# Part of a depthwise convolution moved between engines, with its diagonal weights loaded instead of built

## The reference

```python
z = h @ w_in
cv_v, cv_g, lr_x, lr_y, q, k, v, g_lr, og = split(z)
u = cv_v * sigmoid(cv_g)
u = causal_dw_conv(u, conv_dw_w, conv_dw_b)        # 256 channels, 31 taps
u = silu(layer_norm(u, conv_ln_g, conv_ln_b))
r = rg_lru(...) * gelu(lr_y)                       # a scan over time
o = gla_chunked(q, k, v, lg)                       # 4 heads, chunks of 64
o = rms_norm(o, gla_norm_g) * silu(og)
return concatenate([u, r, o]) @ w_out
```

## Time and profile before

| | us |
|---|---|
| median of three runs | 2743.56 |
| lowest and highest | 2742.04, 2745.74 |
| the profiled execution | 2746.38 |
| its span, from first to last instruction | 2744.6 |
| TensorE busy | 2668.8 (97%) |
| VectorE busy | 2007.4 (73%) |
| ScalarE busy | 1472.0 (54%) |
| GpSimd busy | 192.6 (7%) |

### The profile page before, as it was taken

One profiled execution on the slowest core, in us unless ns is written; L12 is line 12 of the kernel. 1 busy time (PEld: TensorE's weight loads), 2 busy tenths in 40 slices (PEclk: granted clock), 3 DMA queues, 4 the chain that ended last, 5 costly groups with the idle time before them and its releaser, 6 DMA issues.

```text
span 2744.6 us, 46143 instructions
## 1 busy us (share of the span) xinstructions
PE 2668.8 (97%) x15974; PEld 2316.1 (84%) x15974; DVE 2007.4 (73%) x2985; ACT 1472.0 (54%) x2290; POOL 192.6 (7%) x70
## 2 busy tenths in 40 slices
PE   5999899998999999999999999999999999999999
PEld 3766778887999877788899987999887888899987
DVE  7755699998998576743799847899466653699954
ACT  3253489986554356743555525555346753555532
POOL 1441124430000000000000000000000000000000
PEclk9999899999999999999999999999999999999999
DMA  7740599993332241123233232332232123323232
GB/s 287 277 144 31 190 336 412 412 393 115 107 98 89 99 161 57 51 78 114 93 108 104 86 115 79 109 105 90 96 117 106 53 76 109 100 93 107 92 100 100
DMA packets 95470, 376.63 MB, mean 137 GB/s; under 512 B 10800, under 2 KB 11072, under 8 KB 93120
## 3 DMA queue, kind: packets, MB, share of 16 engines
q1 hardware_dynamic: 89584, 348.69, 35.7%
q0 software_dynamic: 4320, 15.73, 1.4%
q10 hardware_dynamic: 1456, 10.74, 1.0%
HBM read 363.59 MB, written 15.73 MB: 138 GB/s over the span
## 4 chain that ended last, share of the span: by engine, by line
PE 84%; DVE 7%; issue 4%; ACT 3%; DMA 0%; POOL 0%; ACTq 0%; DVEq 0%; POOLq 0%
PE pb L1456 15%; PE pb L1458 15%; PE pb L1457 15%; PE pb L1901 10%; PE pb L1903 10%; PE pb L1902 10%; PE pb L2092 1%; PE pb L2124 1%; PE pb L2048 1%; PE pb L1535 1%; ACT SP L1338 1%; DVE hid L2846 1%; PE pb L2101 1%; DVE SP L3023 0%; PE pb L1740 0%
## 5 line engine op out<-in xcount | busy, mean ns | idle before, releaser
L1901 PE MATMUL pb<-bl,g_wh 128*128 128x256 f32 x2464 | 701.9, 285 | 11.0 <-DVE bl L2757 6.9
L1902 PE MATMUL pb<-bh,g_wl 128*128 128x256 f32 x2464 | 697.8, 283 | 0.0
L1903 PE MATMUL pb<-bh,g_wh 128*128 128x256 f32 x2464 | 697.8, 283 | 0.0
L1901 PEld LDWEIGHTS pb<-bl,g_wh 128*128 128x128 f32 x2464 | 473.3, 192 | 15.9 <-issue 9.7
L1902 PEld LDWEIGHTS pb<-bh,g_wl 128*128 128x128 f32 x2464 | 473.6, 192 | 1.6 <-issue 1.4
L1903 PEld LDWEIGHTS pb<-bh,g_wh 128*128 128x128 f32 x2464 | 473.5, 192 | 0.0
L2796 DVE TENSOR_TENSOR w_lo<-raw,w_hi 128x1024 fp32r<-128x1024 f32 x160 | 195.5, 1223 | 186.3 <-ACT w_hi L699 185.2
L1456 PE MATMUL pb<-hl,w_hi 128*128 128x512 f32 x688 | 285.6, 415 | 13.4 <-DVE hl L2255 9.8
L699 ACT ACTIVATE w_hi<-raw 128x1024 fp32r<-128x1024 f32 x186 | 195.9, 1057 | 189.3 <-PE pb L1458 175.4
L1458 PE MATMUL pb<-hh,w_hi 128*128 128x512 f32 x688 | 269.9, 392 | 0.0
L1457 PE MATMUL pb<-hh,w_lo 128*128 128x512 f32 x688 | 269.9, 392 | 0.0
(11 more groups left out here) (488 smaller groups left out, 5551.6 us busy)
## 6 DMA issues: line engine op xcount, KB each, us to landing
raw<-in_wstream SPq DMA_DIRECT2D x220, 512.0 KB, 3.3
m_raw<-in_moe_stream SPq DMA_DIRECT2D x96, 512.0 KB, 8.7
g_own<-in_gu_stream SPq DMA_DIRECT2D x44, 768.0 KB, 4.2
raw<-in_gu_stream SPq DMA_DIRECT2D x44, 768.0 KB, 4.2
m_first<-in_moe_stream SPq DMA_DIRECT2D x48, 512.0 KB, 7.1
hf<-in_moe_stream SPq DMA_DIRECT2D x48, 512.0 KB, 6.6
ada_ring<-in_ada SPq DMA_DIRECT2D x8, 2048.0 KB
g_own<-in_gu_stream SPq DMA_DIRECT2D x44, 256.0 KB, 3.1
```

What stands on the lines that cost most here:

```text
L1901: pe.matmul(o, lh, rl, start=first and k == 0, stop=False, skip_group_check=True)
L1902: pe.matmul(o, ll, rh, start=False, stop=False, skip_group_check=True)
L1903: m = pe.matmul(o, lh, rh, start=False, stop=k == 3, skip_group_check=True)
```

## The change

- VectorE now does 21 taps of the second tile instead of 18. They stand in five groups (3, 5, 5, 4, 4, `EARLY`) right behind the modulation's last step, while the input projection is still running, and no longer behind the states. `PE_TAPS` gives TensorE ten.
- Between the groups VectorE makes the four low halves of pairs 9 and 10, which GpSimd made.
- The 41 diagonals come ready from DRAM, `conv_diag`, made on the host as a layout of the weights. The sync queue loads them to `diag` between the chunks of pairs 9 and 10. GpSimd builds none.
- TensorE does one tap of the second tile between the two key-value groups, six (up to `FILL`) behind the second, none between the heads, one between the last two head statistics and two behind the last.
- The first sum over the channels with ones moves from in front of the output projection into its first tile, behind three of that tile's seven columns.

```diff
-PE_TAPS = (CONV_K, 13)
-DIAG = tuple((t, k) for t in range(NU) for k in range(0, PE_TAPS[t], TAPS))
+PE_TAPS = (CONV_K, 10)
+FILL = 7
+N_DIAG = sum(PE_TAPS)
+EARLY = (3, 5, 5, 4, 4)
...
-            stream((ADA - ADA1) // ADA_EACH, C_WOUT // 2 + 1)
+            n_ada = (ADA - ADA1) // ADA_EACH
+            stream(n_ada, n_ada + 2)
+            sp.wait_ge(ada_used, n_ada)
+            sp.dma_start(diag[:, 0:N_DIAG, :], conv_diag).then_inc(diag_ready, 16)
+            stream(n_ada + 2, C_WOUT // 2 + 1)
...
             low(j0, 1)
-            for i, (j, s) in enumerate(((j0 + 1, 0), (j0 + 1, 1), (j0 + 2, 0))):
-                diagonals(i, i + 1)
-                low(j, s)
-            diagonals(3, len(DIAG))
-            low(j0 + 2, 1)
             pool.wait_ge(xh_ready, 1)
...
                 if p == 1:
+                    pe.wait_ge(conv_out, 1)
+                    conv(1, 0, 1)
                     pe.wait_ge(sc_ready, 2)
...
-            pe.wait_ge(conv_out, 1)
-            conv(1, 0, TAPS)
+            conv(1, 1, FILL)
...
                 m.then_inc(gla_mm, 1)
-                conv(1, TAPS + h, TAPS + h + 1)
                 if h >= 1:
                     head_rms(h - 1)
-            conv(1, TAPS + GH, PE_TAPS[1])
+            conv(1, FILL, FILL + 1)
             head_rms(GH - 1)
+            conv(1, FILL + 1, PE_TAPS[1])
...
-            for t in range(NU):
-                pe.wait_ge(conv_out, t + 1)
-                m = pe.matmul(pb[0][:], ones, z[:, Z_CG + t, :], start=t == 0, stop=t == NU - 1)
-            m.then_inc(ln_mm, 1)
             pe.wait_ge(o_ready, GH)
...
-                out_tile(i, range(1, KD))
+                if i == 0:
+                    out_tile(0, (1, 2, 3))
+                    pe.wait_ge(o_root, 1)
+                    for t in range(NU):
+                        pe.wait_ge(conv_out, t + 1)
+                        m = pe.matmul(pb[0][:], ones, z[:, Z_CG + t, :], start=t == 0, stop=t == NU - 1)
+                    m.then_inc(ln_mm, 1)
+                    out_tile(0, range(4, KD))
+                else:
+                    out_tile(i, range(1, KD))
...
+            dve.wait_ge(u_ready, 2)
+            k = PE_TAPS[1]
+            for i, n in enumerate(EARLY):
+                taps(k, n)
+                k += n
+                if i < 4:
+                    j, half = C_WOUT // 2 - 2 + i // 2, i % 2
+                    dve.wait_ge(w_lod, 2 * j + half)
+                    dve.wait_ge(w_hid, 2 * j + half + 1)
+                    dve.tensor_tensor(w_lo[half][:], raw[half][:], w_hi[half][:].bitcast(F32), ALU.subtract).then_inc(w_lod, 1)
```

More of the change, by code:

```diff
@@ L189, with build @@
     ("ident", P), ("ones", P), ("pairs", P), ("upto", P), ("iota", P), ("chunk_mask", T)])
-def build(nc, xT, cond, ada, wstream, gu_stream, vecs, lvecs, const, masks, lru_gates, gla_gate, moe_stream, na_bias, sw_bias, h_rows, y_rows, out):
+def build(nc, xT, cond, conv_diag, ada, wstream, gu_stream, vecs, lvecs, const, masks, lru_gates, gla_gate, moe_stream, na_bias, sw_bias, h_rows, y_rows, out):
     ctx = ExitStack()
@@ L648, in put @@
                                         ).then_inc(y_out, 16)
-            def diagonals(first, end):
-                for t, k in DIAG[first:end]:
-                    n, w = CONV_K * t + k, min(TAPS, PE_TAPS[t] - k)
-                    pool.tensor_tensor(diag[:, n:n + w, :], ident.unsqueeze(1).broadcast_to([P, w, P]),
-                                       V("conv_w", n, w).unsqueeze(2).broadcast_to([P, w, P]), ALU.mult).then_inc(diag_ready, 1)
             j0 = C_WOUT // 2 - 3
@@ L659, in _ @@
             low(j0, 0)
-            pool.wait_ge(con_in, 16)
-            pool.wait_ge(vec_in, 48)
-            pool.wait_ge(ada_used, (ADA - ADA1) // ADA_EACH)
             low(j0, 1)
-            for i, (j, s) in enumerate(((j0 + 1, 0), (j0 + 1, 1), (j0 + 2, 0))):
-                diagonals(i, i + 1)
-                low(j, s)
-            diagonals(3, len(DIAG))
-            low(j0 + 2, 1)
             pool.wait_ge(xh_ready, 1)
@@ L1532, in conv @@
                 for k in range(first, end):
-                    if k % TAPS == 0 or k == first:
-                        pe.wait_ge(diag_ready, -(-CONV_K // TAPS) * t + k // TAPS + 1)
                     m = pe.matmul(pb[7][:], diag[:, CONV_K * t + k, :], u_pad[:, t, k:k + T], start=k == 0, stop=k == CONV_K - 1,
@@ L1540, in _ @@
             pe.wait_ge(u_ready, 2)
+            pe.wait_ge(diag_ready, 16)
             conv(0, 0, TAPS_1)
@@ L2331, in _, with taps @@
             dve.tensor_tensor(shifted_w, router_w, modv[:, 32:32 + KD].unsqueeze(2).broadcast_to([P, KD, 20]), ALU.mult).then_inc(mod_ready, 1)
+            def taps(first, n):
+                for k in range(first, first + n):
+                    u, w = u_pad[:, 1, k:k + T], V("conv_w", CONV_K + k)
+                    if k == PE_TAPS[1]:
+                        ins = dve.tensor_scalar(hidf[:], u, w, None, ALU.mult)
+                    else:
+                        ins = dve.scalar_tensor_tensor(hidf[:], u, w, hidf[:], ALU.mult, ALU.add)
+                    if k == CONV_K - 1:
+                        ins.then_inc(u_ready, 1)
+                    else:
+                        step(ins)
+            dve.wait_ge(u_ready, 2)
[8 more added lines that the diff above has]
+                    dve.tensor_tensor(w_lo[half][:], raw[half][:], w_hi[half][:].bitcast(F32), ALU.subtract).then_inc(w_lod, 1)
             dve.wait_ge(consts_or_ov_c_mm, 1)
@@ L2403, in _ @@
             dve.tensor_tensor(mt[:, 0:NR, :], mt[:, 0:NR, :], z[:, Z_LY:Z_LY + NR, :], ALU.mult).then_inc(lru_ready, 1)
-            def tap(k):
-                return u_pad[:, 1, k:k + T], V("conv_w", CONV_K + k)
-            step(dve.tensor_scalar(hidf[:], *tap(PE_TAPS[1]), None, ALU.mult))
-            for k in range(PE_TAPS[1] + 1, CONV_K):
-                ins = dve.scalar_tensor_tensor(hidf[:], *tap(k), hidf[:], ALU.mult, ALU.add)
-                if k == CONV_K - 1:
-                    ins.then_inc(u_ready, 1)
-                else:
-                    step(ins)
             dve.wait_ge(lru_ready, 2)
@@ L3291, in lay_out @@
     gg = head_pad(a["gla_w_gate"][0], DK, GH, 64).reshape(16, 2, P)
-    return dict(cond=a["c"], ada=ada_c.transpose(3, 0, 2, 1).reshape(P, ADA, D),
+    taps = np.zeros((P, N_DIAG, P), f)
+    for t in range(NU):
+        for k in range(PE_TAPS[t]):
+            taps[np.arange(P), CONV_K * t + k, np.arange(P)] = a["conv_dw_w"][0][k, P * t:P * t + P]
+    return dict(cond=a["c"], conv_diag=taps, ada=ada_c.transpose(3, 0, 2, 1).reshape(P, ADA, D),
                 xT=a["x"][0].T.reshape(KD, P, T).transpose(1, 0, 2), wstream=ws, gu_stream=gu_stream, vecs=vecs, lvecs=lv, const=con,
```

## The result

| | before | after |
|---|---|---|
| median of 20 executions each, us | 2742.76 | 2750.06 |
| lowest and highest | 2740.13, 2746.22 | 2736.58, 2752.94 |
| ratio | | 1.002, 95% interval 1.0014 to 1.0026 |
| span of the profiled execution | 2744.6 | 2746.7 |
| its mean granted clock | 0.991 | 0.987 |

The account below looks back on a forecast made before the run. It took two chains ending within 0.05 us at the output projection, TensorE's and the last head's through ScalarE and VectorE, as the bound. Projection -4.8 and ones +1.7 gave -3.1 us: 2740.5 us from 2743.56, range 2736.8 to 2745.0.

Parts of the forecast that it names:

- item 1: VectorE's taps under the projections: 21 at 0.785 us plus four low halves end at 164.7, hidden; no gain by itself.
- (2): Four low halves moved from GpSimd to VectorE under the projections: ready before TensorE's tiles want them, cost 0.
- (3): 41 diagonals by DMA, 2.69 MB in 8.6 us: cost 0; at single-chunk pace 16.9 us and a 2.5 us stall.
- (4): One tap in the 0.52 us wait before the second key-value group: costs 0.87, so TensorE +0.39 us.
- item 5: Four taps fewer behind the second key-value group, 0.87 each: -3.49 us; the wait for the states stays closed by 0.7.
- the clock as an unknown: Granted clock 0.50 in the first expert's products: a shifted rise changes seven matmuls, plus or minus about 1 us.
- (6): Two products with ones leave the line before the output projection, 2.24 us from there: TensorE ready at 238.6.
- (7): Last head ready at 239.1: TensorE waits 0.5 us, and the output projection starts 4.8 us earlier.
- The bound with 1.9: Upper bound in us of the wait before the output projection, if the last head's square pushed ScalarE's pair once.
- (8): Products with ones inside the projection's first tile still cost 1.72 us; following VectorE and ScalarE work fits behind twelve matmuls.
- The rivals: For the whole kernel: more gain, 2737.6 us, chance 0.16; nothing arrives, 2743.6, 0.14; slower, 0.06.
- The slower one: Under the projections VectorE fails to keep the tiles' pace, TensorE waits: up to 2753.3 us; chance 0.06.

Follow-up runs that it names:

- e4: Before with only the upstream part: 18 early VectorE taps, four low halves on VectorE, 44 diagonals by DMA; TensorE's order unchanged. 2743.56 us, ratio 0.9992 to 1.0009.
- e1: After with three taps moved back behind the first three heads, two from in front, one from between the last statistics. 2742.34 us, ratio 0.9994 to 1.0017.
- e2: Before with its four taps from between the heads moved: one before the last head statistic, the others behind it. 2750.29 us, ratio 1.0008 to 1.0033.
- e7: After with two useless tap-size products added behind each of the first three heads. 2746.17 us, ratio 1.0011 to 1.0029.
- e5: After with its ten TensorE taps rearranged: four behind the second key-value group, one inside each of four heads, one behind the last statistic. 2742.19 us.
- e6: After with an eleventh TensorE tap: five behind the second key-value group, one behind each of four heads, one behind the last statistic. 2744.33 us.
- e8: After with its ten TensorE taps rearranged: five behind the second key-value group, one inside each of the first three heads, one last. 2742.54 us.
- e10: After with an eleventh TensorE tap: five behind the second key-value group, one inside each of four heads, one behind the last statistic. 2743.54 us.
- e9: Same as e8, but the first products with ones back in front of the output projection. 2738.63 us, ratio to before 0.9975 to 0.9993.
- e12: After with only the first products with ones put back in front of the output projection; heads still bare. 2749.44 us, ratio 1.0011 to 1.0031.
- e3: After with one useless tap-size product added behind each of the first three heads. 2743.44 us, ratio 0.9997 to 1.0015.

## Why the prediction was wrong

**VectorE's taps (item 1): right.** 0.78 a tap for 0.785. VectorE waits 7.14 behind them, where the end at 164.7 in front of 171.8 meant 7.1.

**Low halves (2) and diagonals (3): right at cost 0.** TensorE has no wait under the projections. The transfer took 9.8 us for the 8.6 that I had put, between the two ends, nearer to the cheap one, and neither ScalarE nor TensorE waited for what was queued behind it. e4 shows the sum of the three (with 18 taps for 21), 0 within 0.09%.

**The tap in the wait (4): right.** The wait of 0.52 is gone, and the second group starts 1.88 after the first. Before it was 0.82 and the wait, about 1.4; so +0.48 for +0.39. The states behind it were no bound in after, as item 5 said with 0.7 us to spare: in e1, with two taps less in front of the heads, TensorE waits 0.87 for them.

**Four taps fewer (5), at 0.87 each: here it failed.** The number was right for the taps and wrong for what was between them. They stood in the heads, whose own rows I left at the price of the earlier trace rows without a word on why the price should hold: the sum put the effect of the bare heads on the clock at nothing. Without the taps the granted clock fell to 0.50 in most executions (16 of 20 by the mean clock), and a block then took 1.50 for 0.87, 10.4 us over the heads and what stands behind them. Bare blocks aren't dear by themselves: after's first and all those in e2's trace, with the clock up, take 0.87. The prediction named the clock as an unknown, but looked for it only in the first expert's products, where a 0.50 stood in the trace already. The stretch at 0.50 by the router is there in every trace, and the distance from the second use of the ones to the first expert keeps its length (83.71, 83.81).

**The ones leave the line (6), and what is late next (7): right where the clock is up.** The wait in front of the projection was 0.36 in after and in e7, for the 0.5 of the sum. The bound with 1.9 is what e5, e6, e8 and e10 have, 1.74 and 1.75, since one tap instead of two is left behind the last statistic to cover the last head, and ScalarE's pair is pushed by the one before it.

**The ones inside (8): right in the arithmetic.** In e7, at full clock, the sum of all items is -2.9 for the -3.1 forecast. But the choice was the wrong one of two: with the last head late the ones in front fill its wait, 35.85 in e9 for 37.65 in e8. In after's own order the difference is small: the wait they would fill is 0.36, and e12 is 0.37 shorter than after, both with the clock down.

**The rivals.** The slower one had 0.06 and the wrong mechanism: VectorE kept the pace. None of the rivals was that the removal of a tap could slow the products around it. The four executions of after with a mean clock of 0.990 or more have a median of 2742.8, that of before; four that lie 8.6 us apart neither show nor refute the forecast's gain, which rests on e7's trace. Of the range, the upper end counted scatter of 1.4 us above no gain, from three runs of before; after's own executions lie 16 us apart.

## What to carry to other kernels

A product that is taken out from between small ones isn't worth its own duration alone: ask what the small ones cost without it, and whether the trace of before has any stretch of the same kind that stands bare. Where filler work has to be cut, cut it in front of or behind a sparse stretch and leave some within it, as e9 does. And when a change near such a stretch moves the time by a few us with a wide spread, read the mean granted clock of every execution beside its time before reading one trace: e2's only trace shows a kernel that loses nothing, while five of seven of its executions lose 8 us.

## What the runs showed of the hardware

- The granted clock fell to 0.50 while TensorE's rows were back to back, 4.1 us (after), 5.4 us (e12) and 3.5 us (e3) behind the start of the heads' small products. In after it was back 24 us later, behind the last head, when a statistic and a tap had run at half clock; in e3 20 us later, behind the third head.
- By time and mean clock one program has both courses. After: 16 executions around 2750.4, four from 2736.6 to 2745.1; e2: five from 2748.5 to 2753.4, the two others 2739.7 and 2744.5.
- A fall can also be short. In e6 it lasted 3.4 us, and in e1, with a mean clock of 0.992 over the span, as long, over the last two head statistics, which stand directly one behind the other (in e8 and e9 they do so too, at 1.00):

```profile
233.00:236.00 3.00, 3.00 (x11) 1.47 (x10) 0.55 (x1) 0.78 (x2) 0.00 (x0) 0.68 0.00 0
236.00:239.00 3.00, 3.00 (x6) 1.21 (x5) 1.53 (x3) 2.44 (x4) 0.00 (x0) 0.75 0.00 0
```

- A transfer of 2624 KB in one issue took 9.8 us to landing, and five of 512 KB in the same stretch kept their 3.4 us each.
